# Turning the feed-forward state rows one group per down tile instead of all after the first tile

## The reference

```python
xn2 = rms_norm(x, g_ffn)
up = xn2 @ w_up                                   # (rows, 2*2816)
a_up, b_up = up[..., :D_FF], up[..., D_FF:]
a_ext = jnp.concatenate([ffn_past.astype(a_up.dtype), a_up], axis=1)
a_c = causal_dwconv(a_ext, fcw, fcb)              # width 3
x = x + (jax.nn.silu(a_c) * b_up) @ w_down        # (rows, 1024)
return x, k, v, ki, glu_ext[:, -(CONV_W - 1):], a_ext[:, -(FFN_CONV_W - 1):]
```

## Time and profile before

| | value |
|---|---|
| Time of the kernel before, median of 3 executions | 1193.24 us |
| The three executions | 1193.24, 1193.38, 1189.96 us |
| The profiled execution, its own time | 1191.71 us |
| Span of the profiled execution | 1189.9 us |
| Busy of the span: TensorE, VectorE, ScalarE, GpSimd | 92%, 65%, 26%, 15% |
| Mean granted TensorE clock, share of full speed | 0.957 |
| Down stage, from the first `dn` tile to the last store | about 1034 to 1190 us |

### The profile page before, as it was taken

The page is one execution under the profiler, slowest core; times in us unless marked ns, Lnnn a source line. Parts: engine busy times, 40 slices in busy tenths (PEclk is TensorE's granted clock), DMA queues, the critical chain, the costliest instruction groups (busy, mean ns, idle before and its releaser), DMA issues.

```text
span 1189.9 us, 16823 instructions
## 1 busy us (share of the span) xinstructions
PE 1100.3 (92%) x6738; PEld 890.1 (75%) x6738; DVE 773.8 (65%) x1577; ACT 311.0 (26%) x633; POOL 178.4 (15%) x187
## 2 busy tenths in 40 slices
PE   5999999999779999997868899999999999989996
PEld 3667798665567743445544689999999999989996
DVE  5297998688889999979751265585766656622221
ACT  2111243222111134532323314232323222422120
POOL 0011210000011223237577000000000000001111
PEclk9999999999889999995888899999999999999998
DMA  9210550013243534337679322123232332233331
GB/s 309 54 71 2 191 186 1 17 55 127 87 165 117 168 129 167 132 106 228 211 210 347 97 91 63 37 71 107 72 107 72 93 85 78 68 81 92 101 100 29
DMA packets 109607, 134.49 MB, mean 113 GB/s; under 512 B 8081, under 2 KB 76588, under 8 KB 108484
## 3 DMA queue, kind: packets, MB, share of 16 engines
q1 hardware_dynamic: 90997, 76.67, 21.1%
q0 software_dynamic: 13184, 45.42, 12.0%
q10 hardware_dynamic: 5349, 11.34, 2.7%
HBM read 127.89 MB, written 5.51 MB: 112 GB/s over the span
## 4 chain that ended last, share of the span: by engine, by line
PE 66%; DVE 19%; POOL 4%; issue 4%; ACT 4%; DMA 2%; ACTq 0%; DVEq 0%
PE G L1300 13%; PE G L1301 12%; PE G L1302 12%; PE G L1013 7%; PE G L798 7%; PE G L778 5%; POOL vsel L2594 3%; ACT late L2285 2%; DVE hT L1525 2%; DVE odd_taps L1525 2%; DVE junk L1619 2%; DVE ksel L1835 2%; POOL ksel L2594 1%; PE TB L1037 1%; DVE lgat L1837 1%
## 5 line engine op out<-in xcount | busy, mean ns | idle before, releaser
L1300 PE MATMUL G<-xnH,whi 128*128 128x274 f32 x704 | 205.2, 291 | 1.1 <-DVE aext L1992 0.7
L1301 PE MATMUL G<-xnL,whi 128*128 128x274 f32 x704 | 203.5, 289 | 0.0
L1302 PE MATMUL G<-xnH,wlo 128*128 128x274 f32 x704 | 202.9, 288 | 0.0
L1013 PE MATMUL G<-xnT,wring 128*128 128x280 f32 x512 | 137.3, 422 | 10.3 <-ACT nats L2224 5.0
L1923 DVE TENSOR_TENSOR wlo<-wraw,whi 128x2048 fp32r<-128x2048 f32 (+1 forms) x38 | 76.4, 2012 | 91.8 <-ACT whi L2454 91.0
L1300 PEld LDWEIGHTS G<-xnH,whi 128*128 128x128 f32 x704 | 132.4, 188 | 1.8 <-issue 0.9
L1301 PEld LDWEIGHTS G<-xnL,whi 128*128 128x128 f32 x704 | 133.3, 189 | 0.0
L1302 PEld LDWEIGHTS G<-xnH,wlo 128*128 128x128 f32 x704 | 133.1, 189 | 0.0
L1013 PEld LDWEIGHTS G<-xnT,wring 128*128 128x128 f32 x512 | 98.1, 198 | 39.6 <-issue 6.7
L2594 POOL DMA_INDIRECT ksel<-in_cache_k_dram,gather_row x64 | 70.0, 1094 | 324.9 <-DVE gather_row L1787 176.6
L1300 PE MATMUL G<-hfH,whi 128*128 128x274 f32 x352 | 103.4, 294 | 0.0
(11 more groups left out here) (423 smaller groups left out, 2067.9 us busy)
## 6 DMA issues: line engine op xcount, KB each, us to landing
wraw<-in_w_up_dram SPq DMA_DIRECT2D x44, 512.0 KB, 5.1
wring<-in_w_in_dram SPq DMA_DIRECT2D x8, 2048.0 KB, 8.0
wraw<-in_w_down_dram SPq DMA_DIRECT2D x16, 704.0 KB, 4.4
qB<-scr_q SPq DMA_DIRECT2D x32, 256.0 KB, 3.7
wring<-in_w_in_dram ACTq DMA_DIRECT2D x3, 2048.0 KB, 10.4
wring<-in_w_o_dram SPq DMA_DIRECT2D x2, 2048.0 KB, 14.0
toep<-scr_toep SPq DMA_DIRECT2D x1, 2432.0 KB, 15.1
wqi<-in_w_in_dram SPq DMA_DIRECT2D x2, 1024.0 KB, 9.7
```

What stands on the lines that cost most here:

```text
L1013: last = pe.matmul(out[:, i, 0:b - a], w[:, j, c:c + P], x[:, j, a:b], start=(j == 0), stop=(j == depth - 1))
L1300: pe.matmul(out, w_hi, x_hi, start=start, stop=False)
L1301: pe.matmul(out, w_hi, x_lo, start=False, stop=False)
L1302: return pe.matmul(out, w_lo, x_hi, start=False, stop=stop)
```

## The change

The six groups are spread. Group n now comes behind the matmuls of down tile n, for n = 0 to 5, ahead of that tile's `out_trans(n - 1)`. The groups alternate between the two banks of `TB`, and group i waits for the copy of group i - 2 instead of i - 1. On ScalarE the copy of group n moves behind the two `whi` copies that loop n makes for tile n + 2, and ahead of the copies of output tile n. On GpSimd the two stores of `tailn` move from ahead of all output stores to ahead of those of tile 5. The numbers of instructions, their shapes and the two stores stay what they were.

```diff
-        def state_rows():
-
-            pe.wait_ge(S["ua_in"], 3 * NF)
-            for i in range(6):
-                if i >= 1:
-                    pe.wait_ge(S["tail_done"], i)
-                for f in range(4 * i, min(4 * i + 4, NF)):
-                    last = pe.transpose(TB[0:18, 0, (f % 4) * P:(f % 4 + 1) * P], atail[:, f, :], ident)
-                last.then_inc(S["tail_trans"], 1)
+        def state_rows(i):
+
+            if i == 0:
+                pe.wait_ge(S["ua_in"], 3 * NF)
+            if i >= 2:
+                pe.wait_ge(S["tail_done"], i - 1)
+            for f in range(4 * i, min(4 * i + 4, NF)):
+                last = pe.transpose(TB[0:18, i % 2, (f % 4) * P:(f % 4 + 1) * P], atail[:, f, :], ident)
+            last.then_inc(S["tail_trans"], 1)
...
-            if n == 0:
-                state_rows()
+            if n < 6:
+                state_rows(n)
             if n >= 1:
                 out_trans(n - 1)
...
-        for i in range(6):
-            n = min(4, NF - 4 * i) * P
-            act.wait_ge(S["tail_trans"], i + 1)
-            step(act.activation(tailn[:, 4 * i * P:4 * i * P + n], TB[0:18, 0, 0:n], ACT.Copy), S["tail_done"], free=True)
         for n in range(KM - 1):
             for i in (NF + 4 + 2 * n, NF + 5 + 2 * n):
                 if i < len(fblocks):
                     high_weights(i)
+            if n < 6:
+                width = min(4, NF - 4 * n) * P
+                act.wait_ge(S["tail_trans"], n + 1)
+                step(act.activation(tailn[:, 4 * n * P:4 * n * P + width], TB[0:18, n % 2, 0:width], ACT.Copy), S["tail_done"], free=True)
             act.wait_ge(S["y_trans"], KM + n + 1)
...
-        pool.wait_ge(S["tail_done"], 6)
-        pool.dma_start(OUT["p_ffn_conv"][0, 0], tailn[0:FEXT, :]).then_inc(s_out, 16)
-        pool.dma_start(OUT["s_ffn_conv"][0].rearrange("b e c -> (b e) c"), tailn[FEXT:18, :]).then_inc(s_out, 16)
...
         for n in range(KM - 1):
+            if n == 5:
+                pool.wait_ge(S["tail_done"], 6)
+                pool.dma_start(OUT["p_ffn_conv"][0, 0], tailn[0:FEXT, :]).then_inc(s_out, 16)
+                pool.dma_start(OUT["s_ffn_conv"][0].rearrange("b e c -> (b e) c"), tailn[FEXT:18, :]).then_inc(s_out, 16)
             pool.wait_ge(S["y_nat"], KM + n + 1)
```

## The result

The changed kernel takes 1183.94 us (median of 7 executions, 1181.20 to 1185.31), against 1191.15 us for the kernel before in 7 executions of its own (1187.43 to 1193.38). The ratio is 0.9937, with a 95% interval of 0.9922 to 0.9952: 7.5 us less, between 5.7 and 9.3. Direction and mechanism are the forecast ones. The time is not. 1186.8 us was forecast, in a range from 1183.8 to 1190.0. The median stands 2.9 us under the forecast, at the low edge of the range, and the ratio times 1191.15, 1183.6 us, stands just outside it.

What follows compares the result with a forecast made beforehand. TensorE was taken to bound the down stage; hand-over idle of 4.14 us and slow clock of 1.56 us sum to 5.71 us less, so 1192.5 - 5.7 = 1186.8 us, range 1183.8 to 1190.0.

Steps and rivals of the forecast that it cites:

- The reading of the place: Between down tiles 0 and 1, TensorE and ScalarE hand one bank back and forth; state rows cost 8.15 us in all.
- tile distances: Down tile ends after the change: 17.2 us behind tile 0, then 17.8 us apart, 17.55 at tile 5.
- 0.111 us for each transpose left on the path: All 22 state-row transposes stay on TensorE's path behind tiles 0 to 5, 2.44 us together.
- The price of 6.58 us for the hand-over: Pause between tiles 0 and 1 without the slow clock; 4.14 us of it goes, 2.44 us of transposes stays.
- The forecast saving of 5.71 us: Down stage: 8.15 us cost of the state rows less the 2.44 us of transposes that stay; chance 0.84.
- the base: Whole-kernel time the saving is taken from: 1192.5 us, middle of the profiled execution and three timed runs.
- the clock's term: First 14 matmul steps of tile 1 run at granted clock 0.50; 1.56 us, forecast to go.
- weights: Down-stage weight blocks land in time, with 9.3 us of slack; cost nothing, bounds 0 and +1 us.
- issue gaps: Output transposes behind tiles 1 to 5 follow other transposes; 0 to 0.5 us over five boundaries, taken as 0.
- Slower by transposes that lower the clock: Rival: clock falls at all six boundaries of tiles 0 to 5, +3.65 us, 1196.1 us; chance 0.03.
- The clock still falling at the first boundary, or new issue gaps: Rival at down-tile boundaries: 1.56 or 0.5 us stay, giving 1188.4 or 1187.3 us; chance 0.10 together.
- The wait that moves to the weights: Rival: TensorE in the down stage waits for weights instead; saved 0 to 3 us, about 1191 us; chance 0.03.

Runs made afterwards that it cites:

- six_pauses: Kernel before with the whole six-group block behind each of tiles 0 to 5, GpSimd's two stores ahead of tile 5's; mean 1230.1 us, ratio 1.032.
- repeat8: Changed kernel with every group of transposes run eight times over; 1200.91 us median.
- packed kernel: Changed kernel with 4 transposes instead of 22, all behind tile 0, two copies, eight stores; medians 1182.81, 1183.2 and 1181.76 us.
- null_before_2: The kernel before, no edit, timed once more beside the changed kernel; 1189.51 us median, ratio 0.9993.

## Why the prediction came out as it did

**The reading of the place was right.** The trace of after has the tile distances (17.2, 17.8 and 17.55 us expected; 17.21, 17.76, 17.55 found), and with them 0.111 us for each transpose left on the path. ScalarE's gap is 3.06 us where 3.04 stood before, GpSimd's is 2.51 where 2.4 was expected, and TensorE waited for no weight and no copy. The price of 6.58 us for the hand-over came back in every place of six_pauses that the clock left alone. The forecast saving of 5.71 us was 5.76 in the pair of traces.

**The step that failed first is the base.** The last step of the sum, 1192.5 - 5.7, was set against 1192.5 us, the middle of four executions. The kernel before, over 85 executions in all, has a median of 1190.3 and a mean of 1191.0 us (standard error 0.3). The base was 1.5 to 2.2 us too high, and the low end of the range, the lowest of four values less the saving and another 0.5 us, left no room for that. Against the median 1190.3 the same saving gives 1184.6, where the changed kernel has 1183.5 over 20 executions.

**The second is the size of the clock's term.** The prediction took the 1.56 us of one stretch of one execution as the price of the fall of the clock. The runs showed 0, 1.3, 1.6 and 2.4 us for the same pause, by how long the clock stayed low and how much of that lay in the pause, and 2.0 us in the mean of four traces of the place itself. With that the saving is 6.15 us, and the time 1190.3 - 6.15 = 1184.2 us. The bounds given to the saving were of the wrong terms: weights got up to 1 us and issue gaps up to 0.5, and both turned out at nothing, while the clock got none. That the saving of the first pair of traces was met to 0.05 us is luck in this term.

**The rivals.** Slower by transposes that lower the clock: refuted by the trace of after, with nine in a row, and by repeat8 with 37. The clock still falling at the first boundary, or new issue gaps: neither is in the three traces of the changed kernel. The wait that moves to the weights: the `whi` copy of tile 2's first block moved from 1057.59 to 1054.38, ahead with TensorE, as argued, and TensorE waited for no weight.

**What stays open.** The means over all executions are 1191.0 and 1183.5 us, 7.5 apart with a standard error of 0.5; the medians are 6.8 apart. The traces account for 6.15. Where the 0.7 to 1.3 us beyond come from is not shown. The part of the trace ahead of the down stage doesn't have them (the first addition of the output projection at 710.5 to 713.9 in four traces without the spreading, at 710.8 to 713.5 in three of the changed kernel), and GpSimd's part isn't it.

The clocks on record point at the clock again. Of the executions whose mean granted clock is on record, 78 of the kernel before have 0.9561 and the 20 of the changed kernel 0.9598. The part of full speed that was withheld, times the span, is 52.2 and 47.5 us in the mean, 4.7 apart with a standard error of 0.6. In the four traces of the place the same product around the pause, from 1046 to 1064 us, is only 1.6 to 3.4 us (clock 0.91 to 0.81), 2.5 in the mean. Of the 78, 18 were granted 0.954 or less and took 1194.5 us in the mean, the other 60 took 1189.9; of the changed and the packed kernel together, one of 39 was granted so little. None of those 18 was traced. So it stays open whether the pause cost them more clock than the four traces show, or whether it was lost ahead of the down stage, as in the packed kernel's execution of 1191.74 us, and came to the kernel before more often by chance.

## What to carry to other kernels

When two engines hand one buffer back and forth inside the bound engine's program, a second buffer and a spreading over later work are alternatives: here the second buffer gave 85% of the gain and the spreading all of it. What remains is the number of instructions, which packing columns cuts from 22 to 4. Add the price of the slow steps behind such a pause as a range from nothing to more than one trace shows. And take a kernel's base from its spread, not from three executions, when the gain is half a per cent.

## What the runs showed of the hardware

A pause of 6.6 us, in which TensorE was busy for 3.2 us with 22 short transposes and never idle for more than 0.68 us at a time, left the granted clock at 1.00 in two of six cases within one execution (six_pauses, its second and third). Of the other four, three brought 3.2 to 3.3 us at the lower level and one 6.8. In another execution the clock fell before the pause was over (0.79 over 6.4 us, null_before_2). 37 fp32 transposes in a row between dense matmuls, 4.0 us, left it at 1.00. A transpose of 126 stationary columns takes the same step as one of 18, 0.11 us.
